# Line order of the moving columns and of the results in the weight-unit matmuls of a two-block layer kernel

## The reference, cut to what matters

```python
h = rmsnorm(x, norm_mix[i]);  p = h @ w_in[i]
...
x = x + jnp.concatenate([y_a, y_b, y_c], axis=-1) @ w_out[i]
up = dwconv3(h @ ffn_w_up[i], ffn_conv_w[i], ffn_conv_b[i])
x = x + (jax.nn.silu(gate) * val) @ ffn_w_down[i]
...
proj = h @ w_in
mk, mv = jnp.split(m @ w_mem_kv, 2, axis=-1)
merged = (sigmoid(ga) * (ya @ w_up_a) + sigmoid(gb) * (yb @ w_up_b) + sigmoid(gc) * (yc @ w_up_c))
return x + merged @ w_o
```

## Time and profile before

| | before |
|---|---|
| median of 3 runs | 2315.16 us (2314.85 to 2325.08) |
| span of the profiled execution | 2314.3 us |
| TensorE matmuls | 2298.7 us busy, 99% |
| VectorE | 1529.2 us, 66% |
| ScalarE | 1114.5 us, 48% |
| matmul instructions | 22128 |
| moved by DMA | 401.44 MB |

### The profile page before, as it was taken

One profiled execution on the slowest core, in us unless ns is written; L12 is line 12 of the kernel. 1 busy time (PEld: TensorE's weight loads), 2 busy tenths in 40 slices (PEclk: granted clock), 3 DMA queues, 4 the chain that ended last, 5 costly groups with the idle time before them and its releaser, 6 DMA issues.

```text
span 2314.3 us, 54222 instructions
## 1 busy us (share of the span) xinstructions
PE 2298.7 (99%) x22128; PEld 2264.9 (98%) x22128; DVE 1529.2 (66%) x2109; ACT 1114.5 (48%) x1513; POOL 12.8 (1%) x27
## 2 busy tenths in 40 slices
PE   8999999999999999999999999999999999999999
PEld 7999999999999999999999999999999999999999
DVE  7668767666545666678786677777767555555554
ACT  6443445555434555444644455555546444444442
POOL 0000000000000000000000000000000000000000
PEclk9999999999999999999999999999999999999999
DMA  7553556555555555655554444343434455556554
GB/s 272 168 178 120 181 181 195 187 190 186 187 190 186 188 190 186 223 186 179 195 177 147 132 141 132 129 148 126 135 125 139 163 186 189 190 185 189 190 186 162
DMA packets 110533, 401.44 MB, mean 173 GB/s; under 512 B 12538, under 2 KB 12565, under 8 KB 110240
## 3 DMA queue, kind: packets, MB, share of 16 engines
q1 hardware_dynamic: 108288, 390.91, 51.6%
q0 software_dynamic: 2080, 8.06, 1.1%
HBM read 396.81 MB, written 2.10 MB: 172 GB/s over the span
## 4 chain that ended last, share of the span: by engine, by line
PE 97%; DVE 2%; DMA 0%; issue 0%; ACT 0%; SPq 0%; DVEq 0%; ACTq 0%
PE bank L473 96%; DVE w_lo L1650 1%; DMA raw<-in_units 0%; DVE x L1699 0%; ACT w_hi L1102 0%; PE bank L908 0%; DVE prod L1696 0%; DVE acc L1696 0%; DVE scaled_in L1696 0%; PE bank L834 0%; ACT x L1185 0%; SPq L1067 0%; SPq L1072 0%; DVE fh L1703 0%; PE bank L1009 0%
## 5 line engine op out<-in xcount | busy, mean ns | idle before, releaser
L1650 DVE TENSOR_TENSOR w_lo<-raw,w_hi 128x1024 fp32r<-128x1024 f32 x736 | 894.6, 1223 | 637.4 <-ACT w_hi L1102 632.3
L1102 ACT ACTIVATE w_hi<-raw 128x1024 fp32r<-128x1024 f32 x736 | 778.6, 1059 | 855.2 <-PE bank L473 846.3
L473 PE MATMUL bank<-h_hi,w_hi 128*128 128x256 f32 x4016 | 1134.7, 283 | 8.9 <-DVE h_lo L1699 8.9
L473 PE MATMUL bank<-h_lo,w_hi 128*128 128x256 f32 x4016 | 1121.9, 279 | 0.0
L473 PE MATMUL bank<-h_hi,w_lo 128*128 128x256 f32 x4016 | 1121.2, 279 | 0.0
L473 PEld LDWEIGHTS bank<-h_hi,w_hi 128*128 128x128 f32 x4016 | 755.5, 188 | 15.0 <-DVE h_lo L1699 8.9
L473 PEld LDWEIGHTS bank<-h_lo,w_hi 128*128 128x128 f32 x4016 | 755.7, 188 | 1.6
L473 PEld LDWEIGHTS bank<-h_hi,w_lo 128*128 128x128 f32 x4016 | 755.4, 188 | 0.0
L473 PE MATMUL bank<-m_hi,w_hi 128*128 128x256 f32 x704 | 196.7, 279 | 0.0
L473 PE MATMUL bank<-m_lo,w_hi 128*128 128x256 f32 x704 | 196.5, 279 | 0.0
L473 PE MATMUL bank<-m_hi,w_lo 128*128 128x256 f32 x704 | 196.5, 279 | 0.0
(11 more groups left out here) (434 smaller groups left out, 2734.8 us busy)
## 6 DMA issues: line engine op xcount, KB each, us to landing
raw<-in_units SPq DMA_DIRECT2D x736, 512.0 KB, 3.6
memx<-in_memT POOLq DMA_DIRECT2D x4, 512.0 KB, 8.1
out_y<-obuf SPq DMA_DIRECT2D x8, 256.0 KB, 4.4
x<-in_xT SPq DMA_DIRECT2D x3, 512.0 KB, 9.0
bias_t<-in_bias POOLq DMA_DIRECT2D x8, 192.0 KB, 2.6
dft<-in_dft POOLq DMA_DIRECT2D x1, 1024.0 KB, 10.9
decay<-in_decay POOLq DMA_DIRECT2D x1, 768.0 KB, 7.7
x<-in_xT SPq DMA_DIRECT2D x2, 256.0 KB, 4.5
```

Of the source, the lines that this page charges most:

```text
L473: return pe.matmul(out, lhsT, rhs, start=start, stop=stop, skip_group_check=True)
L1102: return act.activation(out, in_, ACT.Copy, scale=scale)
L1650: dve.tensor_tensor(w_lo[slot][:, :, :], raw[slot][:, :, :], w_hi[slot][:, :, :].bitcast(F32), ALU.subtract).then_inc(split_done, 1)
```

## The change

A function `turned` gives a view of a tile's 256 columns as 64 runs of four neighbours, the last run first. Every weight-unit matmul takes its moving operand and its output through it, so that each result column still lands where it did. Weight operands, the other matmuls, waits and all other engines are as before. Blank lines at the head of the file also go.

```diff
--- before.py
+++ after.py
...
@@ -47,6 +35,7 @@
 RING = 4
 UK = 4
 UN = 256
+LINE = 4
 
 
 U_IN = 17 * 4
@@ -430,6 +419,10 @@
         def out_of(h):
             return banks[OUT[h]][HALVES[h], T:2 * T]
 
+        def turned(ap2d):
+
+            return ap2d.rearrange("p (s e) -> p s e", e=LINE)[:, ::-1, :]
+
         def bcast(ap2d, n):
             return ap2d.unsqueeze(1).broadcast_to([P, n, ap2d.shape[1]])
 
@@ -481,10 +474,11 @@
                     for t in range(tiles):
                         wh = w_hi[slot][:, kk, t * P:(t + 1) * P]
                         wl = w_lo[slot][:, kk, t * P:(t + 1) * P]
-                        rh, rl = hi[:, k0 + kk, :], lo[:, k0 + kk, :]
-                        mm(o[:, t, :], wh, rh, first and kk == 0 and t == 0, False)
-                        mm(o[:, t, :], wh, rl, False, False)
-                        m = mm(o[:, t, :], wl, rh, False, last and kk == UK - 1 and t == tiles - 1)
+                        out = turned(o[:, t, :])
+                        rh, rl = turned(hi[:, k0 + kk, :]), turned(lo[:, k0 + kk, :])
+                        mm(out, wh, rh, first and kk == 0 and t == 0, False)
+                        mm(out, wh, rl, False, False)
+                        m = mm(out, wl, rh, False, last and kk == UK - 1 and t == tiles - 1)
                 m.then_inc(unit_used, 1)
 
             def group(bank, hi, lo, k0=0, units=4, tiles=2, filled=True, arriving=False, ready=None, then=None, after=None):
@@ -655,9 +649,9 @@
                         wl4 = w_lo[slot][:, :, :].rearrange("p k n -> p (k n)").rearrange("p (k n) -> p k n", k=2)
                         for kk in range(2):
                             for t in range(4):
-                                o = p2(pair[t // 2])[:, t % 2, :]
+                                o = turned(p2(pair[t // 2])[:, t % 2, :])
                                 wh, wl = wh4[:, kk, t * P:(t + 1) * P], wl4[:, kk, t * P:(t + 1) * P]
-                                rh, rl = m_hi[:, 2 * u + kk, :], m_lo[:, 2 * u + kk, :]
+                                rh, rl = turned(m_hi[:, 2 * u + kk, :]), turned(m_lo[:, 2 * u + kk, :])
                                 mm(o, wh, rh, u == 0 and kk == 0 and t % 2 == 0, False)
                                 mm(o, wh, rl, False, False)
                                 m = mm(o, wl, rh, False, u == 10 and kk == 1 and t % 2 == 1)
@@ -752,10 +746,11 @@
                     for t in range(2):
                         wh = w_hi[slot][:, kk, t * P:(t + 1) * P]
                         wl = w_lo[slot][:, kk, t * P:(t + 1) * P]
-                        rh, rl = hi[:, (k % 4) * UK + kk, :], lo[:, (k % 4) * UK + kk, :]
-                        mm(o[:, t, :], wh, rh, k % 4 == 0 and kk == 0 and t == 0, False)
-                        mm(o[:, t, :], wh, rl, False, False)
-                        m = mm(o[:, t, :], wl, rh, False, k % 4 == 3 and kk == 3 and t == 1)
+                        out = turned(o[:, t, :])
+                        rh, rl = turned(hi[:, (k % 4) * UK + kk, :]), turned(lo[:, (k % 4) * UK + kk, :])
+                        mm(out, wh, rh, k % 4 == 0 and kk == 0 and t == 0, False)
+                        mm(out, wh, rl, False, False)
+                        m = mm(out, wl, rh, False, k % 4 == 3 and kk == 3 and t == 1)
                 if half != 0:
                     m.then_inc(unit_used, 1)
 
```

## The result

The changed kernel takes 2334.41 us (median of 5 runs, 2333.29 to 2335.42), the kernel before 2316.91 (5 runs, 2314.85 to 2325.08): a ratio of 1.0065, 95% interval 1.0046 to 1.0083; the quotient of the two medians is 1.0076. It is slower, by less than 1%, where 3.2% faster was forecast; the time lies in the stated range, on the other side of the kernel before. Two of the five executions of the kernel before took 2322.41 and 2325.08 us, the other three 2314.85 to 2316.91. The trace, with its span of 2314.3 us, is of a short one, so what the two long ones did isn't shown.

The account below looks back on a forecast made before the run. TensorE's 17,616 weight-unit matmuls, 116.7 ns apart, were taken as the bound; at 112.0 ns they save 82 us, less 1 and 7 lost, 74 us: span 2240, forecast 2241 us, range 2190 to 2410.

Parts of the forecast that it names:

- The bound: Whole kernel: TensorE sets the time, weight-unit matmuls times 116.7 ns between starts; loads and splits are early.
- the matmuls with ones_r: Sign of being right: these 512-column sums, which aren't turned, still take 235 ns each.
- The 112 ns: Weight-unit matmuls: forecast distance between starts after the change, from 116.7 ns, taken from the gvt row of 111.5 ns.
- The floor from the transposes: Rival for weight-unit matmuls: halts go wholly, rhythm of gv transposes, 109 ns; 122 us saved, about 2193 us; chance 0.16.
- The step that failed: Weight-unit matmuls: the turned order of columns and results removes the stream's halts, 116.7 to 112 ns each.
- the same in every unit: Premise for the weak step: the excess of 10.0 ns a matmul doesn't vary between units, as with a fixed address clash.
- The argument against the weight load: 512-column matmuls are 22 ns over, 256-column ones 10.0, so halts lie with moving columns or results, not weight loads.
- The case for no effect: Rival: order doesn't matter to the halts, as mh and m_hi run at the same 116.8 ns; 2315 us, chance 0.22.
- The rival on the slow side: Moving reads or result writes: each jump back costs, 5.4 ns a matmul for 63, 95 us, about 2410 us; chance 0.30.
- The cover in the head loop: Eight head-loop rounds: half of the 14 us gain there is eaten by waits that VectorE's and ScalarE's chains end.
- The term of 7 us: Eight head-loop rounds: part of the 82 us gain counted as lost to VectorE and ScalarE waits, 7 us.
- The 1 us for the start: Before 56 us the chain goes through VectorE, ScalarE and a DMA, with about 192 unit matmuls: 1 us of gain lost.

Follow-up runs that it names:

- one moving column: Kernel before, plain order, each of the 256 moving columns replaced by the first one (step 0), weight loads as they are; 2232.95 us.
- one-column loads: Every unit weight load reads its first column 128 times: on the kernel before 2280.86 us, on the changed kernel 2334.01 us.
- the bank's halves in turn: Kernel before, same work and values, but consecutive matmuls of `unit` write to the two halves of the PSUM bank in turn; 2317.06 us.

## Why the prediction was wrong

**What held.** The bound: distance between starts times 17,616, with the loads, the split and VectorE under cover. TensorE got no new wait, and the matmuls with ones_r, which aren't turned, still start 235 ns apart. That reading costs something also held, but only for half of the excess: of the 10 ns over 106.7, one moving column takes away 5.0 and leaves 5.0. The 112 ns that I took from the matmuls on gvt is within 0.3 ns of what is left, 111.7; that both have the same cause isn't shown, so the match may be luck. The floor from the transposes was not reached by any run, nor the 109.2 ns by the Trainium skill, TensorE: Matmul & The Clock Gate, "Back-to-back issue gap", which gives that formula for an isolated matmul and not for pairs of load and matmul. The rule of the Trainium skill, PSUM — Partial Sum Buffer ("Specifications (TRN2)"), that any non-contiguous pattern slows matmuls significantly doesn't hold for this one: writes in 64 separate runs of four cost nothing.

**The step that failed** is the one the text called weak: "that the turned order removes the halts at all". Nothing stood behind it but that a changed sequence changes the clashes; that was right, and didn't say which way. One of its premises doesn't hold either: the excess isn't "the same in every unit", since 46 of the 601 in the trace before have the slow rhythm. The turned order made 2.800 into 2.827 us a unit, 1.11 ns a matmul, where -4.7 ns was forecast.

**The argument against the weight load was too quick.** From the 512-column matmuls, where I had a weight load cover half the time and the excess doubles all the same, I took the halts to be those of the moving columns or the results. (That half isn't in the row, which has the load 0.19 us long in a step of 0.235.) They do need the moving reads. But the one-column loads changed the plain rhythm (2.800 to 2.720 us in places), and with the moving tiles at one place, byte 192, it is 2.827 us or 2.880 by where the weight tiles lie. A row on how much is lost doesn't say between whom.

**The case for no effect rested on a comparison that could show nothing.** Equal rhythms on m_hi and mh_hi were read as "addresses may not matter". The two tiles start at the same place within 512 bytes, as all moving tiles do, so these rows compare like with like.

**The rival on the slow side had the sign and not the mechanism.** Its price was 5.4 ns for 63 jumps and more for more of them. Measured: nothing for 3, 3.3 ns for 15, 1.1 ns for 63 and for 255. The number of steps in the stride-two transposes was the wrong measure.

**The cover in the head loop.** I had half of the gain eaten there. Of the loss nothing was: the two pieces of a round went from 38.13 and 26.16 to 38.35 and 26.26 us, 0.32 us more, which is 12 units x 0.027 us; 4 of its 16 units had the slow rhythm before. How a gain passes is shown by the kernel with one moving column. Its gain is 0.12 us a unit, and a round of 16 units is 1.93 us shorter, 63.20 for 65.13, so all of it comes through. In the chain the piece of 464 matmuls starts at 1365.39 and again at 1430.52 us before, and with one moving column here:

```profile
1252.86 25.51 PE bank L466 x464
...
1316.06 25.51 PE bank L466 x464
```

The term of 7 us lost there should have been nothing. (The 1 us for the start is small too: 312 unit matmuls stand before 57 us and not 192, 1.5 us at 4.7 ns. The product 17,616 x 4.7 is 83 us, not 82.)

**What stays open** is the machine behind the rhythms: why these orders and places give these values, why a one-column weight load helps in plain order only and not in all stretches, what the 5.0 ns over 106.7 are that stay with one moving column, and what sets the plain stream of the kernel before to 2.827 us between 60 and 164 us. Not every kernel with plain reads is slow there: with the writes alone turned that stretch has 2.800 us, with the bank's halves in turn 2.827. A longer stay at 2.827 us would also give times like the 2322.41 and 2325.08 us of the kernel before, but no trace of such an execution is kept. The rhythm changes over only after other matmuls have come between units, never within an unbroken stream of them; more than that no run shows.

## What to carry to other kernels

Where TensorE is full and its matmuls start further apart than their columns take, first read one moving column over and over, in a copy of the kernel: the difference is what the moving reads cost (here 4.3% of a unit); it needn't be the whole excess. Then vary the offset between moving and stationary tiles in steps of 32 bytes, which costs a pad and no thought, before touching the order of access. Read the starts off the built program and not off the sizes, since each tile is rounded up to a multiple of 32 bytes; a layout edit elsewhere that shifts tiles by 32 or 64 bytes can slow the same code by 0.6 to 2.4%, as here, for no visible reason. Judge an access order only at several placements, since the better of two orders at one offset was the worse at another.

## What the runs showed of the hardware that was not expected

The rhythm of a dense fp32r stream takes fixed values: 2.680, 2.720, 2.800, 2.827, 2.880 and 3.040 us for 24 matmuls, thus 268, 272, 280, 282.7, 288 and 304 cycles of 2.4 GHz for 256 columns. A unit keeps its value within 1 ns (2 ns once in over 11,000) whatever VectorE, ScalarE and the DMA engines do beside it, and from unit to unit, until other matmuls interrupt the stream; the first unit after such an interruption can be up to 30 ns off. One kernel can hold two: plain order shifted by 32 bytes was at 2.827 us except for a few units at 2.720 after such interruptions. Turning the order in which results are written is free: 64 runs backwards into PSUM gave 2.800 us as before.
